# Scratch values kept in PSUM and block pairs mirrored in the head loop of a two-block transformer kernel

## The chip, the cores and the metric

One NeuronCore of a Trainium2 chip runs the kernel. The metric is the device time of one execution in microseconds (us). The engines are TensorE (PE), VectorE (DVE), ScalarE (ACT), GpSimd (POOL) and SyncE (SP), which issues the transfers; SBUF and PSUM are the memories on the chip.

## The reference

256 tokens pass through two transformer blocks of width 1024. The change lies in the second one, in the part that computes, for 16 attention heads of 64 and for 8 recurrent heads of 128:

```python
q = rope(heads(q), pos); k = rope(heads(k), pos)          # t1*cos - t2*sin, t2*cos + t1*sin
p = softmax(where(k_pos <= q_pos, q @ k.T * scale, NEG))   # 256 tokens are one block of the attention
y_a = p @ v
...
fg = lb + (1 - lb) * sigmoid(f);  kh = 1 - fg
b = cumsum(log(fg))                                        # the recurrence in closed form
decay = where(causal, exp(b[t] - b[s]), 0)
a = einsum('td,sd,tsd->ts', silu(q) * dk ** -0.5, kh, decay)
o = a @ i
```

## The kernel before

**The head loop.** The part is a loop of four rounds (`heads2`). A round does four attention heads (two pairs, `j` = 0 to 3) and two recurrent heads (`h` = 0 and 1). Its weights come as 8 chunks of 1 MB, and each chunk gives two output tiles of 128 columns, 16 tiles (`proj(0)` to `proj(15)`), each of 24 matmuls: the weights and the input are split in a high and a low part, ScalarE makes the high part of a chunk in two halves (`ahead2`, L1130), VectorE the low part of the half that is made first (`low_v`, L415) and GpSimd that of the other one (`low_g`, L415).

**The recurrent heads.** The decays between tokens are factored over seven levels, m = 64, 32, ..., 1: within a pair of blocks of m tokens, a key decays to the middle and a query from it. For each level `x` (0 to 6 for head 0, 7 to 13 for head 1) GpSimd writes the differences to the middle (`dl`), ScalarE takes their exponential (`decay`, into `el`, L1429, two buffers), and VectorE multiplies keys (L2027, `kl`) and queries (L2029, `ql`) with it (`level`). TensorE turns them into scores: `hgrn_scores(h, 0)` the diagonal and levels 0 and 1, `(h, 1)` levels 2 to 5, `(h, 2)` level 6 and the product of the two 128-token halves (`cross_level`). A level's scores are block diagonal, and `kl` has zeros for all tokens that are no keys of the level. Every level takes two matmuls, one for each half of the tokens, each with 128 columns of weights and 64 of queries (L930). VectorE puts the scores into the matrix `amat` with predicated copies (`gather0`, `gather1`, `gather2`), and `hgrn_values` multiplies it with the values `iN`.

**The attention heads.** ScalarE copies the tiles of q and k out of PSUM, TensorE multiplies them with a permutation (`rotate`, L894), VectorE applies the sines (`rope_sin`, L2074) and the cosines (`rope_cos`, L2078 and L2079). Then for each head: `scores2` (PE, L903 and L904), `maxima2` (DVE), `exps2` (ACT, L1443 and L1444), `normalise2` (DVE, L2091 to L2093), `turn2` (PE transposes the probabilities, L911), `turned2` (ACT), `values2` (PE).

**What sets the order.** The program of each engine is written out by hand, and an engine does its instructions in that order. Semaphores tie the engines together. `level_ready` counts levels from DVE to PE, `decay_ready` exponentials from ACT to DVE; `turn2(j)` waits for `probs_ready`, and `hgrn_scores(h, 1)` waits until the four levels of its group are done. On TensorE a round stands as: tiles 0 to 5, scores (0, 0), tile 6, rotate q, tile 7, scores (0, 1), rotate k, tile 8, scores (0, 2), tile 9, scores2(0), hgrn_values(0), tile 10, turn2(0), scores2(1), scores (1, 0), tile 11, values2(0), turn2(1), scores2(2), tile 12, scores (1, 1), values2(1), turn2(2), scores2(3), tile 13, scores (1, 2), values2(2), turn2(3), tile 14, hgrn_values(1), values2(3), tile 15.

Of the kernel before, what the change touches and what calls it, by code (L numbers as in the profile page):

```python
# [11 lines left out]
F32 = mybir.dt.float32  # L12
# [6 lines left out]
P = 128  # L19
D = 1024  # L20
KB = D // P
SEQ = 256
# [73 lines left out]
VALUE_BANKS = (6, 2)  # L96
# [68 lines left out]
BODY[('tensor', 'heads2')] = {'roped': 2, 'bank_read7': 4, 'khs_ready': 2, 'level_ready': 16, 'bank_read2': 3, 'bank_read3': 4, 'bank_read4': 4, 'probs_ready': 4, 'bank_read5': 4, 'bank_read6': 1}  # L165
# [3 lines left out]
BODY[('scalar', 'heads2')] = {'bank_full7': 4, 'diff_ready': 14, 'level_ready': 16, 'bank_full4': 4, 'max_ready': 8, 'bank_full3': 4, 'bank_full5': 4, 'bank_full8': 4}  # L169
BODY[('vector', 'heads1')] = {'bank_full4': 4, 'dve_step': 79, 'bank_read4': 4, 'bank_full6': 4, 'conv_ready': 2}  # L170
BODY[('vector', 'up1')] = {'tap0': 8, 'dve_step': 8, 'gate_act': 4}
BODY[('vector', 'heads2')] = {'tanh_ready': 4, 'decay_ready': 16, 'bank_full2': 2, 'dve_step': 22, 'bank_full7': 4, 'bank_read7': 4, 'bank_full3': 4, 'bank_read3': 4, 'bank_full4': 4, 'bank_read4': 4}
# [51 lines left out]
def blocks_kernel(nc, a):  # L224
    ctx = ExitStack()
    with ctx:
# [68 lines left out]
        ones, ident = col("ones", 0, P), col("ident", 0, P)  # L295

# [29 lines left out]
        kh = carve(gluf, 0, HEADS, SEQ)  # L326
        attf = branch[:, :, :].rearrange("p a b -> p (a b)")[:, 2 * KB * TQ:3 * KB * TQ]
# [6 lines left out]
        rope_t = carve(work, 1024, 2, SEQ)  # L334
# [7 lines left out]
        kl = carve(resf, 0, len(LEVELS), SEQ)  # L342
# [3 lines left out]
        el = carve(sqf, 512, 2, SEQ)  # L346
# [39 lines left out]
        meta_shift, meta_exp, meta_probs, meta_T, meta_done = (sem(n) for n in ("meta_shift", "meta_exp", "meta_probs", "meta_T", "meta_done"))  # L386
        att_gated, meta_cleared = sem("att_gated"), sem("meta_cleared")
# [7 lines left out]
        hgrn_ready, tanh_ready, roped = sem("hgrn_ready"), sem("tanh_ready"), sem("roped")  # L395
# [71 lines left out]
        def _(pe):  # L467
# [421 lines left out]
            def rotate(i, src, t):  # L889

                hold(pe, bank_read[2], n.before(bank_read[2]))
                for b in range(2):
                    pe.wait_ge(tile_read[b], STREAM.before("heads2", i, t + b) + 1)
                pe.matmul(ps[:, 2, :], col("rotate", 0, P), src[:, :, :].rearrange("p a b -> p (a b)"),  # L894
                          start=True, stop=True).then_inc(bank_full[2], 1)
# [32 lines left out]
            def level(h, l, bank, at):  # L928
                for blk in range(2):
                    mm = pe.matmul(ps[:, bank, at + HD * blk:at + HD * blk + HD], kl[:, l, blk * P:blk * P + P],  # L930
                                   ql[:, l, blk * HD:blk * HD + HD], start=True, stop=True)
                return mm

            def hgrn_scores(h, g):
# [9 lines left out]
                elif g == 1:  # L944
                    hold(pe, bank_read[3], n.before(bank_read[3]))
# [19 lines left out]
            for b in (2, 3):  # L965
                hold(pe, tile_read[b], STREAM.before("branch_a", 0, b))
            with pe.Fori(0, 4) as i:
# [8 lines left out]
                for t in range(6):  # L976
                    proj(t)
                hgrn_scores(0, 0)
# [35 lines left out]
            for b in VALUE_BANKS:  # L1014
                hold(pe, bank_read[b], n.now(bank_read[b]))
# [80 lines left out]
        def _(sc):  # L1096
# [1454 lines left out]
```

## Time and profile before

| | |
|---|---|
| median of 3 runs | 1180.97 us (1180.48 to 1182.16) |
| the profiled execution | 1181.03 us, its span 1179.4 us |
| granted clock of TensorE, mean | 0.988 |
| busy: PE, DVE, ACT, POOL | 1134.6 us (96%), 720.4 (61%), 600.3 (51%), 651.6 (55%) |
| the chain that ended last | PE 75%, DVE 10%, issue 7%, POOL 5%, ACT 3% |

The span is that of the profiled execution; its own time is the span and 1.6 us around it. Times in the rows are counted from the start of the span. A group of instructions stands with its line, its engine and its operation, out<-in by the names of the memory regions: `work` holds q, k and the probabilities, `res` holds `kl`, `sq` holds `ql`, `dl` and `el`, `glu` the keys `kh`, `act` the matrix `amat`, `ps` is PSUM. An fp32 matmul stands as two records, so that x16 for L930 are eight matmuls; the split products of L570 are one record each.

### The profile page before, as it was taken

What the parts mean: (1) busy time and instruction counts of PE and PEld (TensorE: products, weight loads), DVE (VectorE), ACT (ScalarE), POOL (GpSimd) and SP (SyncE); (2) the same over time, 40 slices, a digit from 0 to 9 for tenths busy, and PEclk for the clock granted to TensorE, in tenths of its full rate; (3) what the DMA queues carried; (4) which work ended last, traced back from release to release, by engine and by line L of the source; (5) the groups of instructions that cost most, each with busy time, mean ns of one, the idle gap of its engine ahead of it and who ended that gap; (6) DMA issues with size and microseconds to landing.
All of it is one profiled execution on the core that took longest, in us unless ns stands there. A gap on an engine that the chain in (4) does not pass through costs nothing.

```text
span 1179.4 us, 24897 instructions
## 1 busy us (share of the span) xinstructions
PE 1134.6 (96%) x8962; PEld 1092.2 (93%) x8962; DVE 720.4 (61%) x1364; ACT 600.3 (51%) x1112; POOL 651.6 (55%) x453
## 2 busy tenths in 40 slices
PE   6999999999889999999899999999999999999997
PEld 6999999998779999999899989898989989999996
DVE  5675766789647777426775757666666546444322
ACT  5654444455256666437545455554635455444332
POOL 5666767660255666544753637364475437656642
PEclk9999999999989999999999999999999999999998
DMA  8444443441344555543432423333445425555541
GB/s 325 144 154 141 171 141 143 143 152 69 142 179 144 178 178 178 199 159 108 178 143 109 142 107 115 134 129 122 160 161 179 143 103 184 181 181 202 185 143 36
DMA packets 26209, 179.43 MB, mean 152 GB/s; under 512 B 2848, under 2 KB 4128, under 8 KB 4768
## 3 DMA queue, kind: packets, MB, share of 16 engines
q1 hardware_dynamic: 25856, 178.28, 42.1%
q8 instruction: 43, 0.70, 0.2%
q10 hardware_dynamic: 288, 0.27, 0.1%
q14 instruction: 22, 0.18, 0.0%
HBM read 177.49 MB, written 1.05 MB: 151 GB/s over the span
## 4 chain that ended last, share of the span: by engine, by line
PE 75%; DVE 10%; issue 7%; POOL 5%; ACT 3%; DVEq 0%; DMA 0%; POOLq 0%; ACTq 0%
PE ps L570 50%; PE ps L852 10%; POOL parts L415 3%; PE ps L930 2%; PE ps L636 1%; DVE ps L2186 1%; DVE act L1824 1%; PE ps L485 1%; ACT parts L1130 1%; DVE branch L1965 1%; PE ps L923 1%; POOL sq L2316 1%; PE ps L610 1%; POOL res L2411 1%; DVE work L1731 1%
## 5 line engine op out<-in xcount | busy, mean ns | idle before, releaser
L415 POOL TENSOR_TENSOR parts<-ring,parts 128x1024 fp32r<-128x1024 f32 x208 | 513.8, 2481 | 468.7 <-ACT parts L1130 465.8
L570 PE MATMUL ps<-x_high,parts 128*128 128x256 f32 (+2 forms) x3088 | 418.0, 284 | 4.3 <-POOL parts L415 2.2
L570 PEld LDWEIGHTS ps<-x_high,parts 128*128 128x128 f32 x3088 | 387.5, 189 | 15.5 <-issue 7.1
L1130 ACT ACTIVATE parts<-ring 128x1024 fp32r<-128x1024 f32 x324 | 323.9, 1049 | 138.3 <-PE ps L852 69.3
L415 DVE TENSOR_TENSOR parts<-ring,parts 128x1024 fp32r<-128x1024 f32 x116 | 152.6, 1315 | 127.3 <-ACT parts L1130 127.3
L570 PE MATMUL ps<-x_low,parts 128*128 128x256 f32 (+2 forms) x1520 | 214.5, 284 | 0.0
L570 PEld LDWEIGHTS ps<-x_low,parts 128*128 128x128 f32 x1520 | 196.3, 189 | 0.0
L1751 DVE SCALAR_TENSOR_TENSOR ps<-glu,table_sb,ps 128x256 f32<-128x256 f32 x232 | 93.3, 481 | 0.6 <-DVE ps L1751 0.3
L852 PE MATMUL ps<-act_high,parts 128*128 128x256 f32 x704 | 87.8, 279 | 0.0
L852 PEld LDWEIGHTS ps<-act_high,parts 128*128 128x128 f32 x704 | 85.1, 188 | 0.0
L570 PE MATMUL ps<-parts,x_high 128*128 128x256 f32 x448 | 62.3, 285 | 0.9 <-DVE work L2099 0.9
L570 PEld LDWEIGHTS ps<-parts,x_high 128*128 128x128 f32 x448 | 56.4, 188 | 3.0 <-issue 3.0
L1109 ACT ACTIVATE work<-ps 128x256 f32<-128x256 f32 (+2 forms) x52 | 20.0, 386 | 74.9 <-PE ps L570 71.9
L852 PE MATMUL ps<-act_low,parts 128*128 128x256 f32 x352 | 46.5, 282 | 0.0
L852 PEld LDWEIGHTS ps<-act_low,parts 128*128 128x128 f32 x352 | 43.8, 189 | 0.0
L1100 ACT ACTIVATE work<-work 128x256 f32<-128x256 f32 x44 | 18.3, 418 | 49.0 <-DVE work L2276 33.0
L1100 ACT ACTIVATE work<-ps,table_sb 128x256 f32<-128x256 f32 x44 | 24.5, 559 | 33.3 <-PE ps L570 29.6
L1965 DVE TENSOR_TENSOR branch<-work 128x256 f32 (+1 forms) x22 | 34.4, 1563 | 3.8 <-DVE work L1960 2.3
L2434 POOL TENSOR_TENSOR sq<-conv 128x128 f32 x56 | 25.6, 457 | 19.6 <-ACT sq L1429 16.0
L1100 ACT ACTIVATE sq<-res 128x256 f32<-128x256 f32 (+2 forms) x48 | 18.2, 412 | 34.9 <-DVE res L1874 27.6
L485 PE MATMUL ps<-conv,ring 128*128 128x258 f32 x128 | 30.4, 399 | 3.5 <-DVE x_high L1837 3.5
L2027 DVE TENSOR_TENSOR res<-glu,sq 128x128 f32<-128x128 f32 x56 | 31.4, 560 | 3.8 <-ACT sq L1429 2.6
(333 smaller groups left out, 1602.2 us busy)
## 6 DMA issues: line engine op xcount, KB each, us to landing
ring<-weights SPq DMA_DIRECT2D x166, 1024.0 KB, 4.8
res<-h_in SPq DMA_DIRECT2D x4, 272.0 KB, 3.6
act<-mem SPq DMA_DIRECT2D x1, 1024.0 KB, 14.6
out<-xT SPq DMA_DIRECT2D x4, 256.0 KB, 2.4
table_sb<-table SPq DMA_DIRECT2D x1, 969.5 KB, 8.9
table_sb<-table ACTq DMA_DIRECT2D x1, 132.5 KB, 3.5
work<-positions ACTq DMA_DIRECT2D x1, 128.0 KB, 5.5
```

The costliest lines, as they stand in the source:

```text
L415: eng.tensor_tensor(parts[:, LOW - HIGH + p, cols], ring[:, slot, cols], parts[:, p, cols].bitcast(F32), ALU.subtract)\
L485: mm = pe.matmul(ps[:, b, 0:width], ring[:, slot, k * CW + e * P:k * CW + e * P + P], moving(k), start=k == 0, stop=k == KB - 1)
L570: mm = pe.matmul(out, left(k), right(k), start=step_ == 0 and k == 0, stop=step_ == 2 and k == KB - 1)
L852: mm = pe.matmul(ps[:, DOWN_BANK + t // 2, t % 2 * SEQ:(t % 2 + 1) * SEQ], w[:, kk * D + t * P:kk * D + t * P + P], x[:, kb + kk, 0:SEQ], ...
L930: mm = pe.matmul(ps[:, bank, at + HD * blk:at + HD * blk + HD], kl[:, l, blk * P:blk * P + P], ql[:, l, blk * HD:blk * HD + HD], start=Tru ...
L1100: ins = sc.activation(out, src, fn, **kw)
L1109: sc.activation(out, src, fn, scale=scale).then_inc(tile_read[b], 1)
L1130: sc.activation(parts[:, p, cols], ring[:, slot, cols], ACT.Copy).then_inc(split_high, 1)
L1751: ve.scalar_tensor_tensor(acc, u, w, acc, ALU.mult, ALU.add).then_inc(dve_step, 1)
L1965: ve.tensor_tensor(branch[:, j + (e - 2), 0:SEQ], silu_g[:, 2 * (g % 2) + e - 2, :], acc, ALU.mult)\
L2027: ve.tensor_tensor(halves(kl[:, l, :], m)[:, :, 0, :], halves(kh[:, i * 2 + h, :], m)[:, :, 0, :], e[:, :, 0, :], ALU.mult)
L2434: gp.tensor_tensor(d[:, :, 0, :], middle, b[:, :, 0, :], ALU.subtract)
```

## The change

- **Mirrored levels.** The second 128 tokens of the keys are written in reversed order, so that the keys of both halves of a level fill one block of 128 tokens without zeros. A level takes one matmul with 128 columns of queries. VectorE writes the keys in two instructions of 64 elements (L2050 and L2051 of the changed kernel) and the queries in one of 128 (L2052).
- So that values stand in the same order, TensorE multiplies the second half of `iN` with a reversed identity (`mirror_values`, after tile 4), and ScalarE copies it back. ScalarE makes `kh_s` in four instructions of 128 elements instead of two of 256.
- **PSUM.** The exponentials of the decays go to PSUM bank 2, which is one buffer (`el` was two): an exponential waits until the level before it is done. The rotated halves are multiplied with the sines in PSUM (bank 6), all of the rope in one piece (`rope`). The exponentials of the attention heads stay in PSUM bank 4.
- **Order.** On TensorE tile 9 stands ahead of scores (0, 2), and tile 10 ahead of `hgrn_values(0)`. On VectorE `rope(q_r)` and `gather0` stand ahead of level 5, `low_v` of chunk 6 between `maxima2(0)` and `normalise2`, level 13 and `cross_level` ahead of `normalise2` of head 2, `gather1` ahead of that of head 3, and `cumulate` at the end.
- GpSimd's clearing of `kl` before the loop falls away. VectorE makes the mirrored masks and the two identities once, between two low parts of the phase `down1`, with 15 small instructions.

```diff
-VALUE_BANKS = (6, 2)
+VALUE_BANKS = (6, 6)
+DECAY_BANK, TURN_BANK = 2, 6
...
+            def mirror_values(i):
+
+                b = STREAM.bank("heads2", 3)
+                hold(pe, bank_read[TURN_BANK], n.before(bank_read[TURN_BANK]))
+                pe.wait_ge(tile_read[b], STREAM.before("heads2", i, 3) + 1)
+                pe.matmul(ps[:, TURN_BANK, 0:CW], both_diagonals[:, P:2 * P], iN[:, 1, :], start=True, stop=True)\
+                  .then_inc(values_mirrored, 1)
...
             def level(h, l, bank, at):
-                for blk in range(2):
-                    mm = pe.matmul(ps[:, bank, at + HD * blk:at + HD * blk + HD], kl[:, l, blk * P:blk * P + P],
-                                   ql[:, l, blk * HD:blk * HD + HD], start=True, stop=True)
-                return mm
+                return pe.matmul(ps[:, bank, at:at + P], kl[:, l, :], ql[:, l, :], start=True, stop=True)
...
-                for t in range(6):
+                for t in range(5):
                     proj(t)
+                mirror_values(i)
+                proj(5)
                 hgrn_scores(0, 0)
...
                 proj(8)
+                proj(9)
                 hgrn_scores(0, 2)
-                proj(9)
                 scores2(0)
+                proj(10)
                 hgrn_values(0)
-                proj(10)
                 turn2(0)
...
                 sc.wait_ge(diff_ready, n.next(diff_ready))
-                reuse(x)
-                sc.activation(el[:, x % 2, :], dl[:, x % 2, :], ACT.Exp).then_inc(decay_ready, 1)
+                reuse(0)
+                sc.activation(ps[:, DECAY_BANK, 0:SEQ], dl[:, x % 2, :], ACT.Exp).then_inc(decay_ready, 1)
...
-                e = halves(el[:, x % 2, :], m)
-                ve.tensor_tensor(halves(kl[:, l, :], m)[:, :, 0, :], halves(kh[:, i * 2 + h, :], m)[:, :, 0, :],
-                                 e[:, :, 0, :], ALU.mult)
+                e, keys = halves(ps[:, DECAY_BANK, 0:SEQ], m), halves(kh[:, i * 2 + h, :], m)
+                b = P // (2 * m)
+                ve.tensor_tensor(halves(kl[:, l, :], m)[:, :, 0, :], keys[:, 0:b, 0, :], e[:, 0:b, 0, :], ALU.mult)
+                ve.tensor_tensor(halves(kl[:, l, :], m)[:, ::-1, 1, ::-1], keys[:, b:, 0, :], e[:, b:, 0, :], ALU.mult)
...
-            def rope_sin(bank):
-                ve.wait_ge(bank_full[bank], n.next(bank_full[bank]))
-                ve.tensor_tensor(rope_t, ps[:, bank, :].rearrange("p (a t) -> p a t", t=SEQ), wide(sin), ALU.mult)\
-                  .then_inc(bank_read[bank], 1)
-
-            def rope_cos(x):
-                step(ve.tensor_tensor(x, x, wide(cos), ALU.mult))
-                ve.tensor_tensor(x, x, rope_t, ALU.add).then_inc(roped, 1)
+            def rope(x):
+                z = ps[:, TURN_BANK, :].rearrange("p (a t) -> p a t", t=SEQ)
+                ve.tensor_tensor(x, x, wide(cos), ALU.mult)
+                step(ve.tensor_tensor(z, z, wide(sin), ALU.mult))
+                ve.tensor_tensor(x, x, z, ALU.add).then_inc(bank_read[TURN_BANK], 1)
...
                 low_v("heads2", i, 4)
                 level(i, 0, 4)
-                rope_sin(2)
+                ve.wait_ge(rotated, n.next(rotated))
+                rope(q_r)
+                gather0()
                 level(i, 0, 5)
-                gather0()
-                rope_cos(q_r)
+                ve.wait_ge(rotated, n.next(rotated))
+                rope(k_r)
                 level(i, 0, 6)
                 cross_level(i, 0)
                 low_v("heads2", i, 5)
+                level(i, 1, 7)
                 gather1()
-                rope_sin(2)
-                rope_cos(k_r)
-                gather2()
-                level(i, 1, 7)
                 level(i, 1, 8)
-                if scan:
-                    ve.wait_ge(log_ready, 2)
-                    cumulate(i + 1)
+                gather2()
                 maxima2(0)
-                normalise2()
                 low_v("heads2", i, 6)
+                normalise2()
                 maxima2(1)
```

The first place is VectorE between the fourth and the fifth level of head 0. Before, the row of the sines (L2074) is followed by level 5 (L2027 and L2029), the diagonal and the first two predicated copies, and then the cosines:

```order
L2074 TENSOR_TENSOR work<-ps,work 128x512 [waits bank_full2]
L2025 REGISTER_ALU
L2027 TENSOR_TENSOR res<-glu,sq 128x64x2 [waits decay_ready]
L2029 TENSOR_TENSOR sq<-work,sq 128x128
L221 REGISTER_ALU
L2050 REGISTER_ALU [waits bank_full3]
L2051 TENSOR_TENSOR act<-ps,table_sb 128x256 [waits bank_full7]
L1639 ISA
L2043 COPY_PREDICATED act<-table_sb,ps 128x2x64 [waits dve_step]
L2046 REGISTER_ALU
L2043 COPY_PREDICATED act<-table_sb,ps 128x4x32 [waits dve_step]
L2078 TENSOR_TENSOR work<-work 128x512 [waits bank_read7]
```
In the changed kernel the whole rope of q (L2096 to L2098) and `gather0` (L2074 and L2066) come first:

```order
L2096 TENSOR_TENSOR work<-work 128x512 [waits rotated]
L2097 TENSOR_TENSOR ps<-ps,work 128x512
L1649 ISA
L2098 TENSOR_TENSOR work<-work,ps 128x512 [waits dve_step]
L222 REGISTER_ALU
L2073 REGISTER_ALU [waits bank_full3]
L2074 TENSOR_TENSOR act<-ps,glu 128x256 [waits bank_full7]
L1649 REGISTER_ALU
L2066 COPY_PREDICATED act<-table_sb,ps 128x2x64 [waits dve_step]
L2069 REGISTER_ALU
L2066 COPY_PREDICATED act<-table_sb,ps 128x4x32 [waits dve_step]
L2047 REGISTER_ALU [waits bank_read7]
```
The last row opens level 5, whose three products (L2050 to L2052) follow it; they have moved behind two more products of 512 elements, one of 256 and two predicated copies.

The second place is VectorE at the first attention head. Before, the maxima (L2084 to L2087) are followed by the probabilities (L2091 to L2093) and those by the low part of chunk 6 (L415):

```order
L2082 REGISTER_ALU
L2084 TENSOR_TENSOR ps<-ps,table_sb 128x2x128 [waits bank_full4]
L1639 REGISTER_ALU
L2086 TENSOR_REDUCE small<-ps 128x1 [waits dve_step]
L2087 TENSOR_REDUCE small<-ps 128x1
L2090 REGISTER_ALU
L2091 RECIPROCAL small<-small 128x2 [waits bank_read4]
L1639 REGISTER_ALU
L2092 TENSOR_SCALAR work<-work,small 128x128 [waits dve_step]
L2093 TENSOR_SCALAR work<-work,small 128x256
L414 ISA
L415 TENSOR_TENSOR parts<-ring,parts 128x1024 [waits split_high]
```
In the changed kernel the low part (L417) stands between them:

```order
L2101 REGISTER_ALU
L2103 TENSOR_TENSOR ps<-ps,table_sb 128x2x128 [waits bank_full4]
L1649 REGISTER_ALU
L2105 TENSOR_REDUCE small<-ps 128x1 [waits dve_step]
L2106 TENSOR_REDUCE small<-ps 128x1
L416 ISA
L417 TENSOR_TENSOR parts<-ring,parts 128x1024 [waits split_high]
L2109 REGISTER_ALU
L2110 RECIPROCAL small<-small 128x2 [waits bank_read4]
L1649 REGISTER_ALU
L2111 TENSOR_SCALAR work<-ps,small 128x128 [waits dve_step]
L2112 TENSOR_SCALAR work<-ps,small 128x256
```
The row that waits for `split_high`, the high part of chunk 6, has moved ahead of the rows that `turn2(0)` waits for.

## Rows read from the trace of the kernel before

**Rows 1.** Busy time by stretch (us): one round of the head loop.

```profile
649.40:714.80 65.40, 65.40 (x511) 60.61 (x510) 43.43 (x99) 34.99 (x77) 32.91 (x37) 1.00 0.36 128
```

**Rows 2.** The chain that ended last, head loop: start us, us, engine, line, records.

```profile
635.94 20.10 PE ps L570 x168
656.04 0.44 PE ps L940 x4
...
663.90 1.73 PE ps L930 x16
...
673.74 0.63 PE ps L960 x2
...
701.30 20.10 PE ps L570 x168
```

**Rows 3.** Timeline of TensorE, one round: start us, us, engine, line, operation.

```profile
660.05 1.02 PE L894 MATMUL ps<-work,table_sb 128*128 128x512 f32 x2
...
663.74 1.89 PE L930 MATMUL ps<-sq,res 128*128 128x64 f32 x16
...
672.82 0.48 PE L903 MATMUL ps<-work 64*128 64x128 f32 x2
...
677.28 0.49 PE L911 MATMUL ps<-table_sb,work 128*128 128x128 f32 x3
...
690.62 0.55 PE L911 MATMUL ps<-table_sb,work 128*128 128x128 f32 x3
...
696.46 0.55 PE L911 MATMUL ps<-table_sb,work 128*128 128x128 f32 x3
```

**Rows 4.** Timeline of VectorE, same round.

```profile
661.11 0.69 DVE L2074 TENSOR_TENSOR work<-ps,work 128x512 f32<-128x512 f32 x1 [1.72 <-PE ps L894]
...
662.46 0.41 DVE L2051 TENSOR_TENSOR act<-ps,table_sb 128x256 f32<-128x256 f32 x1
...
663.82 0.69 DVE L2078 TENSOR_TENSOR work<-work 128x512 f32<-128x512 f32 x1
664.54 0.78 DVE L2079 TENSOR_TENSOR work<-work 128x512 f32<-128x512 f32 x1
665.24 0.28 DVE L2027 TENSOR_TENSOR res<-glu,sq 128x128 f32<-128x128 f32 x1
665.45 0.28 DVE L2029 TENSOR_TENSOR sq<-work,sq 128x128 f32<-128x128 f32 x1
...
673.97 0.41 DVE L2084 TENSOR_TENSOR ps<-ps,table_sb 128x256 f32<-128x256 f32 x1
...
676.01 0.17 DVE L2091 RECIPROCAL small<-small 128x2 f32<-128x2 f32 x1 [0.98 <-ACT work L1444]
...
676.41 0.35 DVE L2093 TENSOR_SCALAR work<-work,small 128x256 f32<-128x256 f32 x1
676.96 1.23 DVE L415 TENSOR_TENSOR parts<-ring,parts 128x1024 fp32r<-128x1024 f32 x1 [0.20 <-ACT parts L1130]
...
696.04 1.77 DVE L2043 COPY_PREDICATED act<-table_sb,ps 128x128 f32<-128x128 int32 x4
```

**Rows 5.** Timeline of ScalarE, same round.

```profile
660.53 0.41 ACT L1429 ACTIVATE sq<-sq 128x256 f32<-128x256 f32 x1
...
675.07 0.37 ACT L1443 ACTIVATE work<-ps,small 128x128 f32<-128x128 f32 x1 [1.75 <-DVE small L2087]
...
675.87 2.00 ACT L1130 ACTIVATE parts<-ring 128x1024 fp32r<-128x1024 f32 x2
```

**Rows 6.** Timeline of all engines, same round: GpSimd beside VectorE.

```profile
652.75 2.49 POOL L415 TENSOR_TENSOR parts<-ring,parts 128x1024 fp32r<-128x1024 f32 x1 [1.50 <-ACT parts L1130]
...
653.63 1.76 DVE L2027 TENSOR_TENSOR res<-glu,sq 128x128 f32<-128x128 f32 x1 [0.64 <-ACT sq L1429]
...
659.61 2.38 POOL L415 TENSOR_TENSOR parts<-ring,parts 128x1024 fp32r<-128x1024 f32 x1
```

**Rows 7.** Timeline of VectorE in the phase down1.

```profile
489.14 1.23 DVE L415 TENSOR_TENSOR parts<-ring,parts 128x1024 fp32r<-128x1024 f32 x1 [4.45 <-ACT parts L1130]
```

More of the change, by code:

```diff
@@ L889, in rotate @@
             def rotate(i, src, t):
[L891 removed]
+                hold(pe, bank_read[TURN_BANK], n.before(bank_read[TURN_BANK]))
                 for b in range(2):
                     pe.wait_ge(tile_read[b], STREAM.before("heads2", i, t + b) + 1)
[L894 to L895 removed]
+                pe.matmul(ps[:, TURN_BANK, :], col("rotate", 0, P), src[:, :, :].rearrange("p a b -> p (a b)"),
+                          start=True, stop=True).then_inc(rotated, 1)
+            def mirror_values(i):
+                b = STREAM.bank("heads2", 3)
+                hold(pe, bank_read[TURN_BANK], n.before(bank_read[TURN_BANK]))
+                pe.wait_ge(tile_read[b], STREAM.before("heads2", i, 3) + 1)
+                pe.matmul(ps[:, TURN_BANK, 0:CW], both_diagonals[:, P:2 * P], iN[:, 1, :], start=True, stop=True)\
+                  .then_inc(values_mirrored, 1)
             def scores2(j):
@@ L900, in scores2 @@
                 if j == 0:
-                    pe.wait_ge(roped, n.next(roped, 2))
+                    hold(pe, bank_read[TURN_BANK], n.now(bank_read[TURN_BANK]))
                 hold(pe, bank_read[4], n.before(bank_read[4]))
@@ L1013, in _ @@
             last_products = split_late("branch_a", ya_high, ya_low, SEQ, None, 2)
-            for b in VALUE_BANKS:
-                hold(pe, bank_read[b], n.now(bank_read[b]))
+            hold(pe, bank_read[VALUE_BANKS[1]], n.now(bank_read[VALUE_BANKS[1]]))
             last_products()
@@ L1507, in _ @@
                 copy2(9, vA[:, 1, :])
+                decay(8)
                 exps2(0)
@@ L2134, in heads2 @@
                 low_v("heads2", i, 5)
+                level(i, 1, 7)
                 gather1()
-                rope_sin(2)
-                rope_cos(k_r)
+                level(i, 1, 8)
                 gather2()
-                level(i, 1, 7)
-                level(i, 1, 8)
+                maxima2(0)
+                low_v("heads2", i, 6)
+                normalise2()
+                maxima2(1)
+                gather0()
+                normalise2()
+                for x in range(9, 13):
+                    level(i, 1, x)
+                maxima2(2)
+                level(i, 1, 13)
+                cross_level(i, 1)
+                normalise2()
+                low_values(i, 0)
+                low_v("heads2", i, 7)
+                maxima2(3)
+                gather1()
+                normalise2()
+                gather2()
                 if scan:
@@ L2143, in heads2 @@
                     cumulate(i + 1)
-                maxima2(0)
-                normalise2()
-                low_v("heads2", i, 6)
-                maxima2(1)
-                normalise2()
-                gather0()
-                for x in range(9, 13):
-                    level(i, 1, x)
-                maxima2(2)
-                normalise2()
-                level(i, 1, 13)
-                cross_level(i, 1)
-                low_values(i, 0)
-                low_v("heads2", i, 7)
-                maxima2(3)
-                normalise2()
-                gather1()
-                gather2()
                 low_v("heads2", i, 8)
```

57 lines of the change are left out of this document (33 added, 24 removed).

## The prediction

> **What bounds the kernel now.** I first read the busy time by stretch. One round of the head loop shows TensorE busy for 65.40 of 65.40 us at a granted clock of 1.00, VectorE for 43.43, ScalarE for 34.99 and GpSimd for 32.91 [rows 1]. Then the chain that ended last: it stays on TensorE through the loop, and the same piece stands at 635.94 and at 701.30, so a round is 65.36 us [rows 2]. All that VectorE, ScalarE and GpSimd do is covered, and a change pays only through TensorE's own work. The question is then how far ahead of TensorE the others are, which only the timelines tell. VectorE is busy without a gap from 661.11, when the rotated q has come, to the end of the maxima of head 0 at 675.03, just before ScalarE takes them up at 675.07; head 0's probabilities are done at 676.41 + 0.35 = 676.76, and TensorE uses them at 677.28 [rows 3 to 5]. That is 0.5 us of slack in a round of 65.
>
> **What TensorE saves.** Group (h, 1) is eight matmuls of 64 columns in 1.73 us, 0.216 each; a matmul of 128 columns costs the same, two of them in 0.44 us [rows 2]. So the weights set the price, and one matmul for two saves 0.21 us per level. 14 levels save 2.94 us a round. `mirror_values` adds a matmul of 256 columns. The product of that width stands in a piece of 0.63 us that holds its start [rows 2]; the bounds are 0.43 (half of the 512 columns that L894 takes in 0.86) and 0.63, and I take 0.5. Net: 2.4 us a round saved, 9.8 us over four rounds, if TensorE still never waits. It reads `iN` one whole tile (20.10 us for seven, 2.87 [rows 2]) after tile 3, which ScalarE copies at once, so that this matmul itself waits for nothing.
>
> **Where it will wait.** I lay the new program over the round of the rows, with the durations of its rows, and keep their clock.
>
> Early levels. The single buffer turns a level into a round trip: exponential 0.41 [rows 5], products 0.56 (0.14 + 0.14 + 0.28; two products of 128 start 0.21 apart [rows 4], so that one of 64 takes 0.14), and two hand-overs of 0.03: about 1.04 us. Levels 0 to 4 have the gaps for it, level 4 being done near 659.8, and group (0, 0) has over 3 us of slack.
>
> Level 5. TensorE now arrives at group (0, 1) at 663.8, as before at 663.74 [rows 3] (0.5 added, 0.4 saved). The rotated q reaches VectorE near 661.2. Then come the cosines, the sines and the sum (0.61 to 0.72 each, 2.0 together, from L2074, L2078 and L2079), `gather0` (from 662.46 to 663.82, 1.36) and level 5 (0.55): done 3.9 us after 661.2, at 665.1, if nothing is in its way. That alone is a wait of 1.3 us.
>
> But the cosines are a product of two SBUF operands. Such a product, started at 653.63 while GpSimd was in its low part of 652.75 to 655.24, took 1.76 us instead of 0.28, till just behind its end [rows 6]. L2074, which has one operand in PSUM, took its normal 0.69 in the middle of the low part of 659.61 to 661.99 [rows 4, 6]. The new level products are of that free kind, the cosines are not. GpSimd's low part of chunk 4 waits behind a difference that waits for the exponential of level 4, and comes at about 660.1 to 662.5. The cosines end at 662.5 + 0.5, the sum and `gather0` at 665.7, level 5 at 666.3. TensorE waits 2.4 us (bounds 1.2 and 2.6). Behind that wait stands `rotate` of k, for which VectorE waits in turn.
>
> Head 0. `rotate` ends by 668.3. GpSimd's next low part, behind the difference that needs level 5's successor, starts near 667.6, so the cosines of k are held until 670.1 too. Rope ends at 672.0; level 6 and `cross_level` (1.0) are just ahead of TensorE, which comes to (0, 2) at 673.8. Then `low_v` 1.15, level 7 0.55, `gather1` 1.8 (four copies in 1.77 [rows 4]), level 8 0.55, `gather2` 0.7: VectorE begins `maxima2(0)` at 677.75 and ends at 678.85. The scores have been there since 675.1. From the end of the maxima the old trace took 0.98 us to the probabilities' first row (676.01) and 0.75 more to their end. Now the low part of chunk 6 is between, and it waits for the high part, which ScalarE makes only behind those exponentials: from 675.03 (end of the maxima) to 676.96 (start of L415) are 1.93 us [rows 4, 5], L415 costs 1.15, `normalise2` 0.75: 3.8 us. Probabilities at 682.7. TensorE is at `turn2(0)` at 678.75 and waits 3.9 us. The bound from below: were VectorE free when the scores come, as it was, the path is 1.1 + 3.8 = 4.9 us against the 3.6 that TensorE has to do between (677.28 less 672.82 + 0.85 [rows 3]), so that 1.4 us stay in any case.
>
> Second half, counted from `turn2(0)` as T. Head 1 is in time: probabilities at T + 4.6, wanted at T + 5.9. Levels 9 to 12 at one per 1.04 us end at T + 8.3, which is when the scores of head 2 are just there (T + 7.2); `maxima2(2)` follows to 9.4, exponentials 10.35, and then level 13 and `cross_level`, which ScalarE can feed only now, stand ahead of `normalise2`: T + 12.5, wanted at T + 11.9 (before 690.62 less 677.28, 13.3 [rows 3], now 1.3 to 1.4 less for six saved matmuls of 0.21). Wait 0.6, bounds 0 and 1.0. For head 3 the low part of chunk 7 (VectorE free at T + 14.1, held by GpSimd's to 15.6, done 16.7), the maxima to 17.7, `gather1` 1.85 behind them instead of the 0.95 of the exponentials, and `normalise2`: T + 20.3. TensorE is there at T + 18.1 (696.46 less 677.28 [rows 3], 19.2, less seven times 0.21 and a little, plus the 0.6). Wait 2.2, bounds 0.8 (the low part not held) and 2.5.
>
> Sum: waits 2.4 + 3.9 + 0.6 + 2.2 = 9.1 us a round, less 2.4 saved, 6.7 more; four rounds 26.8. Against the profiled execution's own 1181.03 us, which is the median of the runs within 0.1, that is 1207.8.
>
> Edits at nothing: the exponentials and probabilities in PSUM are as long as before (L2074 with PSUM and L2078 without both take 0.69 us for 512 elements [rows 4]). The 15 instructions in `down1`, at 0.2 to 0.3 us like other short rows, are some 4 us in a stage where VectorE waits 4.45 us between two low parts [rows 7]; without that cover they would cost up to 4 us once. Four ScalarE copies for two add 0.4 us at a place where `decay(2)` has room. The clearing of `kl` was before the loop and beside TensorE's products.
>
> One rule of the Trainium skill speaks against the change. "VectorE: DVE Perf Modes", its section on the TRN2 errata, gives an instruction from PSUM a fixed 120 cycles and one from SBUF 58. By it an estimate is 0.065 us more for each product that now reads PSUM, twelve of which stand between the rope of q and `maxima2(0)`: 0.8 us a round more, 1211. The rows of equal length above say otherwise, and I go by them.
>
> **The rivals.** *The ports don't matter (15%).* If GpSimd's low parts fall elsewhere, the cosines are free. Then level 5 is done at 665.1, a wait of 1.2; VectorE ends `maxima2(0)` at about 675.9, which makes 2.2 at `turn2(0)`; 0.6 and 0.8 behind: 4.8 less 2.4, 2.4 a round, 1191. For it: a shift of 1 us decides each of the three. Against it: each of the low parts hangs on what VectorE and ScalarE did just before.
>
> *Both near their lower bounds (7%).* 1.2 and 1.4 and nothing behind are 2.6 against 2.4: no change, 1181 to 1183.
>
> *Faster (11%).* VectorE is fast enough after all. The point that decides is level 5 by 663.8 and probabilities within 3.6 us of the scores. It takes products of 64 elements and ropes in PSUM that are much shorter than their relatives in the rows, 3.9 us falling to 2.6. Nothing in the rows speaks for it, but it would give all that TensorE saves: 1171.
>
> *Worse (7%).* The waits push ScalarE's high parts too, which I have behind TensorE's needs by a microsecond or two only at chunk 0 of the next round: another 1 to 3 us a round, 1212 to 1220.
>
> **How the numbers follow.** My forecast, 1195 to 1212, has 60%; its likeliest is 1208. The waits' bounds alone would give from 1.2 + 1.4 to 2.6 + 4.2 + 1.0 + 2.5 = 10.3 less 2.4, 1182 to 1213. The range that leaves out less than 2 in 10 is 1184 to 1214: it takes in the second case and leaves the faster one, most of the unchanged one and half of the worse one. A measurement of this kernel tells about 0.2%, 2.4 us, from no change. Slower by more than that: 60 + 15 + 7 and nothing of the rest, 0.82; within it 0.07; faster 0.11.
>
> **What would show it.** In the changed kernel L939 stands as 112 matmul records of 128 columns, a group of four in about 0.88 us. Rows in which TensorE is idle until VectorE: at group (0, 1) on the products of level 5, and at the transposes of the probabilities on L2112, in every round, the latter the longest. L2096 should have members well over 0.69 us, L2050 to L2052 none over 0.3. A round is 72 us instead of 65.4. I am wrong if TensorE is gapless in the loop, or if the idle time lies at the start of tiles, on weights' parts.

## The result, and the profile after

The changed kernel takes 1219.18 us (median of 4 runs, 1216.15 to 1221.96) against 1181.07 (1180.48 to 1182.16): ratio 1.0314, 95% interval 1.0287 to 1.0341. It is slower by 38 us; 27 were forecast. Its profiled execution took 1216.15 us (span 1214.5, mean granted clock 0.973).

Busy time by stretch, one round of the changed kernel (as [rows 1]: PE, PEld, DVE, ACT, POOL, granted clock, share of the DMA engines, GB/s):

```profile
674.73:749.63 74.90, 67.93 (x482) 61.84 (x483) 42.61 (x112) 35.54 (x82) 30.27 (x36) 0.93 0.32 113
```

A round takes 74.90 us against 65.40 [rows 1]. VectorE is busy no longer than before (42.61 against 43.43); TensorE is idle for 6.97 us, and its clock is 0.93 instead of 1.00. The waits of TensorE from 560 to 880 us, in all, times, longest:

```profile
PE ps L921 <- DVE work L2112: 17.4, 8, 2.7
PE ps L939 <- DVE sq L2052: 9.0, 4, 2.3
```

L939 waits for the products of level 5, L921 (the transposes of the probabilities of heads 0 and 3) for L2112, the end of `normalise2`. These are three of the four places that were forecast; at `turn2(2)` TensorE does not wait here. The timeline of TensorE, around the three waits of the round:

```profile
674.73 1.23 PE L939 MATMUL ps<-sq,res 128*128 128x128 f32 x8 [2.27 <-DVE sq L2052]
675.76 1.92 PE L896 MATMUL ps<-work,table_sb 128*128 128x512 f32 x2
676.69 2.63 PE L572 MATMUL ps<-parts,x_high 128*128 128x256 f32 x8
...
688.65 0.38 PE L970 MATMUL ps<-act,work 128*128 128x128 f32 x2
691.69 0.55 PE L921 MATMUL ps<-table_sb,work 128*128 128x128 f32 x3 [2.66 <-DVE work L2112]
...
705.36 0.55 PE L921 MATMUL ps<-table_sb,work 128*128 128x128 f32 x3
...
713.06 0.79 PE L921 MATMUL ps<-table_sb,work 128*128 128x128 f32 x3 [2.04 <-DVE work L2112]
713.50 2.06 PE L572 MATMUL ps<-x_high,parts 128*128 128x256 f32 x8
```

The durations behind the waits have grown. Eight products of L572 take 2.63 us behind the first wait; the same group takes 1.50 us where the clock is full (674.02 in a fence of experiment 5). Busy time by stretch shows why, in its third last column (the first two rows belong to the round before):

```profile
616.00:620.00 4.00, 2.88 (x11) 2.07 (x12) 1.75 (x7) 0.93 (x3) 2.41 (x1) 0.71 0.22 35
620.00:624.00 4.00, 4.00 (x21) 4.00 (x21) 2.64 (x11) 1.19 (x5) 0.81 (x2) 0.50 0.57 229
...
676.00:680.00 4.00, 4.00 (x18) 2.97 (x18) 2.29 (x2) 0.00 (x0) 3.25 (x4) 0.61 0.00 0
680.00:684.00 4.00, 4.00 (x36) 4.00 (x35) 3.82 (x13) 0.69 (x2) 1.09 (x2) 1.00 0.00 0
...
692.00:696.00 4.00, 4.00 (x20) 3.30 (x18) 1.51 (x5) 1.68 (x6) 1.09 (x2) 0.59 0.47 131
...
712.00:716.00 4.00, 2.94 (x15) 2.94 (x16) 3.42 (x11) 2.04 (x3) 0.00 (x0) 0.65 0.50 209
```

Behind each of the three waits TensorE is busy again at a granted clock of 0.50, its lower level of 1.2 GHz, for about 3.4 us in this round, and then returns to 2.4 GHz: 1.7 us of work are lost each time. Behind two waits of the other rounds (2.59 us, ending at 617.12, and 2.32, ending at 839.19) it is nearly 7 us, with 3.4 lost. In the kernel before, the loop has 1.00 throughout, in this round [rows 1] and in the other three: it had no waits.

VectorE and GpSimd around the first two waits:

```profile
669.66 1.77 DVE L2096 TENSOR_TENSOR work<-work 128x512 f32<-128x512 f32 x1 [1.45 <-PE ps L896]
...
674.40 0.28 DVE L2052 TENSOR_TENSOR sq<-work,ps 128x128 f32<-128x128 f32 x1
677.71 2.08 DVE L2096 TENSOR_TENSOR work<-work 128x512 f32<-128x512 f32 x1 [3.04 <-PE ps L896]
...
687.21 0.41 DVE L2106 TENSOR_REDUCE small<-ps 128x1 f32<-128x256 f32 x1
689.55 1.23 DVE L417 TENSOR_TENSOR parts<-ring,parts 128x1024 fp32r<-128x1024 f32 x1 [1.93 <-ACT parts L1137]
...
691.15 0.48 DVE L2112 TENSOR_SCALAR work<-ps,small 128x256 f32<-128x256 f32 x1
```
```profile
668.52 2.37 POOL L417 TENSOR_TENSOR parts<-ring,parts 128x1024 fp32r<-128x1024 f32 x1
...
676.89 2.37 POOL L417 TENSOR_TENSOR parts<-ring,parts 128x1024 fp32r<-128x1024 f32 x1
```

Both cosines (L2096) end just behind a low part of GpSimd, at 671.4 and 679.8. Those of q do so in every round. Those of k take 1.58, 2.08 and 2.27 us in the three rounds in which the clock falls behind the first wait, and 0.73 in the last round, in which it doesn't (the wait of 2.18 us that ends at 824.19). In `normalise2` the low part of chunk 6 waits 1.93 us for ScalarE's high part, exactly as long as was read from before. By form, from 600 to 880 us, cosines, queries' products and the larger product of the normalisation (busy, mean ns, idle before):

```profile
L2096 DVE TENSOR_TENSOR work<-work 128x512 f32<-128x512 f32 x7 | 12.0, 1712 | 15.9 <-PE ps L896 15.9
...
L2052 DVE TENSOR_TENSOR sq<-work,ps 128x128 f32<-128x128 f32 x51 | 14.3, 281 | 0.0
...
L2112 DVE TENSOR_SCALAR work<-ps,small 128x256 f32<-128x256 f32 x16 | 7.6, 476 | 0.0
```

### The profile page after: what moved, and what is told of

It is laid out like the page before. It is cut to its first block, busy times and chain, and to the rows that moved or that the text cites. A ratio compares the mean times of both kernels' runs of the same rounds, so it can differ in the third digit from the quotient of the medians.

```text
span 1214.5 us, 24795 instructions
## 1 busy us (share of the span) xinstructions
PE 1141.6 (94%) x8858; PEld 1095.2 (90%) x8858; DVE 720.6 (59%) x1435; ACT 602.1 (50%) x1124; POOL 639.0 (53%) x452
## 4 chain that ended last, share of the span: by engine, by line
PE 64%; DVE 16%; issue 10%; POOL 5%; ACT 4%; DVEq 1%; DMA 0%; POOLq 0%; ACTq 0%; SPq 0%
PE ps L572 43%; PE ps L854 10%; POOL parts L417 3%; ACT parts L1137 2%; PE ps L638 1%; DVE act L2066 1%; DVE parts L417 1%; DVE ps L2205 1%; DVE act L1834 1%; PE ps L487 1%; PE ps L939 1%; DVE branch L1975 1%; PE ps L896 1%; POOL sq L2335 1%; PE ps L612 1%
## 5 line engine op out<-in xcount | busy, mean ns | idle before, releaser
L417 POOL TENSOR_TENSOR parts<-ring,parts 128x1024 fp32r<-128x1024 f32 x208 | 510.7, 2465 | 468.7 <-ACT parts L1137 465.8
L572 PE MATMUL ps<-x_high,parts 128*128 128x256 f32 (+2 forms) x3088 | 424.5, 287 | 2.8 <-POOL parts L417 2.7
L572 PEld LDWEIGHTS ps<-x_high,parts 128*128 128x128 f32 x3088 | 393.3, 191 | 15.3 <-issue 8.4
L417 DVE TENSOR_TENSOR parts<-ring,parts 128x1024 fp32r<-128x1024 f32 x116 | 155.4, 1340 | 144.5 <-ACT parts L1137 144.5
L572 PE MATMUL ps<-x_low,parts 128*128 128x256 f32 (+2 forms) x1520 | 217.3, 286 | 0.0
L572 PEld LDWEIGHTS ps<-x_low,parts 128*128 128x128 f32 x1520 | 199.4, 192 | 0.0
L572 PE MATMUL ps<-parts,x_high 128*128 128x256 f32 x448 | 64.3, 293 | 3.2 <-DVE work L2118 3.2
L572 PEld LDWEIGHTS ps<-parts,x_high 128*128 128x128 f32 x448 | 58.3, 195 | 7.0 <-issue 6.9
L1436 ACT ACTIVATE ps<-sq 128x256 f32<-128x256 f32 x56 | 21.6, 386 | 46.7 <-DVE res L2058 23.7
```

The source lines that it names most:

```text
L417: eng.tensor_tensor(parts[:, LOW - HIGH + p, cols], ring[:, slot, cols], parts[:, p, cols].bitcast(F32), ALU.subtract)\
L572: mm = pe.matmul(out, left(k), right(k), start=step_ == 0 and k == 0, stop=step_ == 2 and k == KB - 1)
L1436: sc.activation(ps[:, DECAY_BANK, 0:SEQ], dl[:, x % 2, :], ACT.Exp).then_inc(decay_ready, 1)
```

## The experiments

Ratios are to runs of the kernel before on the same chip.

### What a wait costs

**1. The waits filled.** Throwaway matmuls of ones and an identity, 9 ahead of the wait at scores (0, 1), 14 and 8 at `turn2(0)` and `turn2(3)`:

```diff
+                for _ in range({0: 14, 3: 8}.get(j, 0)):
+                    pe.matmul(ps[:, 5, 0:P], ones, ident, start=True, stop=True)
                 pe.wait_ge(probs_ready, n.next(probs_ready))
```

> The changed kernel, with throwaway matmuls (ones times identity, 0.21 us each) that TensorE does in the places where it waits: 9 ahead of the wait of group (0, 1), 14 ahead of turn2(0), 8 ahead of turn2(3), in every round. They write to a bank that the next real matmuls overwrite. Theory 1 (the miss of the forecast is the granted clock, which falls behind each wait and makes about 3.4 us of work twice as long): with the waits filled the clock stays at 1.00 in the loop, a round is 72 to 72.5 us, and the kernel takes 1206 to 1211 us although it does more work. Theory 2 (the waits themselves are longer than I reckoned and the clock is only a by-product): the time stays at 1216 to 1222 or grows by what the extra matmuls cost.

Measured: 1203.72 us (1200.84 to 1206.15), 1.0189 (1.0163 to 1.0214). The loop's clock is 1.00 and a round 70.89 us (level group at 671.62 and 742.51):

```profile
671.62 1.16 PE L941 MATMUL ps<-sq,res 128*128 128x128 f32 x8 [0.28 <-DVE sq L2056]
699.85 0.52 PE L923 MATMUL ps<-table_sb,work 128*128 128x128 f32 x3 [0.46 <-DVE work L2116]
742.51 1.16 PE L941 MATMUL ps<-sq,res 128*128 128x128 f32 x8 [0.28 <-DVE sq L2056]
```

More work for TensorE makes the kernel 15.5 us faster. Two things in the trace refine this. The cosines of k (L2100 here) are free: they start just ahead of GpSimd's low part, and GpSimd is the one that takes longer. And 14 matmuls at `turn2(0)` are more than fit: the probabilities are done at 686.14 + 0.48 = 686.62, and the transposes start at 687.26.

```profile
673.68 0.69 DVE L2100 TENSOR_TENSOR work<-work 128x512 f32<-128x512 f32 x1 [2.11 <-PE ps L896]
...
686.14 0.48 DVE L2116 TENSOR_SCALAR work<-ps,small 128x256 f32<-128x256 f32 x1
```
```profile
673.78 2.86 POOL L417 TENSOR_TENSOR parts<-ring,parts 128x1024 fp32r<-128x1024 f32 x1
```
```profile
687.26 0.49 PE L923 MATMUL ps<-table_sb,work 128*128 128x128 f32 x3
```

In the change the transposes start 0.06 us behind the probabilities (691.63 and 691.69). So about 0.6 us of each filled round is the fillers' own (an estimate from these rows): at full clock a round would take some 70.3 us. Of the 38 us the lowered clock, with the hold of k's cosines that comes with it, is then 15.5 us as measured and some 18 without the fillers' excess. The other 20 are what the waits cost less what TensorE saves.

**2. One of the three filled** (14 matmuls, at `turn2(0)` alone).

> The changed kernel with throwaway matmuls at one of its three waits only: 14 of them ahead of the wait for the first probabilities, none at scores (0, 1) or at the probabilities of head 3. The waits themselves (2.3 and 2.0 us of TensorE) stay at the other two places. The run with one low part moved has just these two waits and a granted clock of 1.00 behind both. Theory A (the clock falls behind two of the waits only because of the third between them): the loop shows a clock of 1.00 and a round of about 70.9 us, 1202 to 1206 us, no slower than with all three filled. Theory B (each wait of 2 us or more brings its own stretch of half clock, and the other run escaped by something else in its order): the stretches behind the two waits stay, 1.7 us each, and the time is 1210 to 1218 us.

Measured: 1215.48 us (1212.45 to 1215.73), 1.0274 (1.0252 to 1.0295): theory B's time. But the clock doesn't fall behind every wait:

```profile
600.00:604.00 4.00, 1.73 (x14) 1.53 (x14) 3.29 (x9) 2.44 (x4) 0.00 (x0) 1.00 0.70 254
604.00:608.00 4.00, 4.00 (x30) 3.52 (x30) 2.12 (x5) 0.68 (x3) 3.49 (x5) 1.00 0.02 8
640.00:644.00 4.00, 4.00 (x24) 4.00 (x22) 2.73 (x6) 2.38 (x3) 1.16 (x1) 0.57 0.07 27
676.00:680.00 4.00, 3.76 (x17) 2.95 (x18) 1.36 (x2) 1.12 (x4) 3.05 (x5) 0.70 0.16 66
```

A wait of 2.27 us that ends at 603.79 leaves the clock at 1.00, one of 2.04 ending at 639.70 lowers it, and the next of 2.27, ending at 676.24, lowers it too. Over the loop three of the four waits at scores (0, 1) leave it alone, and all four at `turn2(3)` lower it. The run prices one fall: the round with one (603.79 to 676.24) takes 72.45 us, the round with two (676.24 to 750.24) 74.00, and the filled one 70.89: 1.55 us each, a little less than the 1.7 us of lost work, since later waits shrink.

**3. The late low part in the kernel before**, alone:

```diff
                 maxima2(0)
-                normalise2()
                 low_v("heads2", i, 6)
+                normalise2()
```

> The kernel before with one edit: the low part of chunk 6 stands between maxima2(0) and normalise2(0). By the rows of before the probabilities then come 2.1 us later (678.85) and TensorE waits 1.6 us in each round. Theory 1 (each wait also costs clock, 1.7 us): 1.6 + 1.7 = 3.3 us a round, 1194 us, and a granted clock under 0.99 in the loop. Theory 2 (a wait costs only itself): 1187.5 us. If the slack is taken up elsewhere: 1181.

Measured: 1206.43 us (1205.19 to 1211.14), 1.0221 (1.0192 to 1.0251). One moved line costs 25.4 us, and 13 were expected. VectorE, then GpSimd, then TensorE:

```profile
685.55 1.23 DVE L415 TENSOR_TENSOR parts<-ring,parts 128x1024 fp32r<-128x1024 f32 x1 [1.93 <-ACT parts L1130]
...
686.89 2.17 DVE L2092 TENSOR_SCALAR work<-work,small 128x128 f32<-128x128 f32 x1
```
```profile
686.54 2.43 POOL L415 TENSOR_TENSOR parts<-ring,parts 128x1024 fp32r<-128x1024 f32 x1 [6.04 <-ACT parts L1130]
```
```profile
689.38 0.90 PE L911 MATMUL ps<-table_sb,work 128*128 128x128 f32 x3 [3.34 <-DVE work L2093]
```

Both terms were larger than expected. L2092, with one input and one output in SBUF, is held until GpSimd's low part ends (2.17 us, a mean of 0.29 before), so that the wait is 3.34 us and not 1.6. Behind it the clock is 0.59 and 0.56 for two stretches of 4 us (688 to 696), which loses about 3 us of work and not 1.7.

**4. The same with 15 throwaway matmuls** at `turn2(0)`.

> The kernel before with the low part of chunk 6 ahead of normalise2(0), as in e5_before_low6 (1206.4 us, one wait of 3.34 us a round, granted clock 0.95), plus 15 throwaway matmuls (3.2 us) that TensorE does in place of that wait. If the wait costs itself and the clock behind it the rest: clock 1.00, a round 65.4 + 3.5 = 68.9 us, 1195 us. If the clock is no part of the price: 1206 us.

Measured: 1196.08 us (1195.15 to 1198.76), 1.0115 (1.0093 to 1.0138), the loop's clock 1.00. A round takes 68.99 us against 71.79 in experiment 3. The medians are 10.4 us apart; this run was on another chip, where the kernel before takes 1182.54 us, so that 13.5 of the 25.4 us are left and the clock is 10 to 12.

### Which piece of the order

**5. Low part of chunk 6 back** behind `normalise2` of head 0, in the changed kernel, alone.

> The changed kernel with the low part of chunk 6 put back behind the normalisation of head 0, nothing else. Theory: the wait of 2.7 us at the first transposes falls under 1 us, the waits at scores (0, 1) and of head 3 stay: 2 to 4 us a round less, 1203 to 1211 us. Rival (the low part is only exchanged for another delay at head 3 or at tile 12): less than 1 us a round, 1215 us or more.

Measured: 1195.61 us (1194.84 to 1197.84), 1.0121 (1.0105 to 1.0137), 23.6 us off the change. A round is 68.27 us (672.57 to 740.84), 6.6 less. The wait that shrinks, from 2.66 to 0.29 us, is only 2.4 of them; the rest is the clock:

```profile
672.57 1.16 PE L939 MATMUL ps<-sq,res 128*128 128x128 f32 x8 [2.28 <-DVE sq L2052]
...
674.02 1.50 PE L572 MATMUL ps<-parts,x_high 128*128 128x256 f32 x8
675.36 1.11 PE L572 MATMUL ps<-parts,x_low 128*128 128x256 f32 x8
...
685.53 0.55 PE L921 MATMUL ps<-table_sb,work 128*128 128x128 f32 x3 [0.29 <-DVE work L2112]
...
705.78 0.55 PE L921 MATMUL ps<-table_sb,work 128*128 128x128 f32 x3 [2.03 <-DVE work L2112]
```
```profile
672.00:676.00 4.00, 3.43 (x24) 2.96 (x25) 1.85 (x6) 1.45 (x4) 2.71 (x5) 1.00 0.24 100
...
708.00:712.00 4.00, 4.00 (x30) 3.50 (x30) 1.99 (x3) 1.98 (x4) 2.46 (x1) 1.00 0.00 0
```

Two waits stay, as long as before, and now the clock keeps 1.00 behind both, in all four rounds. Why it does here, and not behind waits as long in the change, no run shows.

**6. Level 5 back** ahead of the rope of q, in the changed kernel, alone.

> The changed kernel with level 5 put back ahead of the rope of q, nothing else. Theory (waits add, and each costs its own length and the half clock behind it): the wait of 2.3 us at scores (0, 1) goes with its 1.7 us of clock, the wait at the first transposes stays near 2.7 us: 3 to 4 us a round less, 1203 to 1208 us. Rival (VectorE is the bound of this stretch, so a wait removed early comes back at the transposes): the wait there grows to over 4 us and the time is 1213 us or more.

Measured: 1210.75 us (1207.06 to 1212.26), 1.0236 (1.0218 to 1.0255), between the times of the two theories. The wait at scores (0, 1) is gone, and the one at `turn2(0)` has grown from 2.66 to 4.01, with half clock for nearly 7 us behind it in three of the four rounds. The lateness is VectorE's: a wait that TensorE no longer has early comes back later. And a hold has moved on: with the cosines of k free (0.69 us), the product of `cross_level` took their place beside a low part of GpSimd:

```profile
678.87 2.49 DVE L2058 TENSOR_TENSOR res<-work,res 128x128 f32<-128x128 f32 x1
```

**7. Both.**

> The changed kernel with two pieces of VectorE's order put back: level 5 ahead of the rope of q, and the low part of chunk 6 behind normalise2(0). Theory 1 (the order on VectorE makes the waits): the wait at group (0, 1) is gone, that at turn2(0) falls to 1.4 us or less, those of the second half stay; 1187 us if the clock cost nothing, 1192 to 1200 with it. Theory 2 (the single buffer of the exponentials makes VectorE late, the order matters little): over 1208 us.

Measured: 1195.79 us (1193.15 to 1201.16), 1.0139 (1.0104 to 1.0173), no faster than 5 alone: the wait of 2.28 at scores (0, 1) has become one of 1.93 at `turn2(0)`, with the clock lowered behind it.

**8. GpSimd's low parts of chunks 4 and 5 one difference earlier.**

```diff
-                for x in (0, 1, "low 2", 2, 3, "low 3", 4, 5, 6, "low 4", 7, 8, "low 5", 9, 10, "low 6", 11, 12, 13,
+                for x in (0, 1, "low 2", 2, 3, "low 3", 4, 5, "low 4", 6, 7, "low 5", 8, 9, 10, "low 6", 11, 12, 13,
```

> The changed kernel with GpSimd's low parts of chunks 4 and 5 one difference earlier in its order, so that they lie ahead of the ropes. Theory 1 (a product of two SBUF operands is held until GpSimd's low part ends): L2096 falls from 1.77 and 2.08 us to 0.7 to 1.3, the wait at group (0, 1) from 2.3 to about 1.4, the one at turn2(0) by about 1, the whole to 1208 to 1213 us. Theory 2 (the ports don't matter, L2096 is slow for another reason): L2096 as long as before, 1216 to 1222 us.

Measured: 1210.13 us (1205.96 to 1211.05), 1.0248 (1.023 to 1.0265).

```profile
666.91 0.79 DVE L2096 TENSOR_TENSOR work<-work 128x512 f32<-128x512 f32 x1 [1.45 <-PE ps L896]
...
673.04 0.90 DVE L2096 TENSOR_TENSOR work<-work 128x512 f32<-128x512 f32 x1 [2.11 <-PE ps L896]
```
```profile
673.36 2.86 POOL L417 TENSOR_TENSOR parts<-ring,parts 128x1024 fp32r<-128x1024 f32 x1
```

With GpSimd elsewhere the cosines are free, and the wait at scores (0, 1) falls from 2.27 to 1.29 us: the hold was about 1 us of that wait, and VectorE's order the rest. The wait at `turn2(0)` was expected to shrink by about 1 us and is 3.00: counted from TensorE's coming to scores (0, 1), the probabilities are ready 2.3 us earlier in the round than in the change, but TensorE comes 2.6 us earlier, since it waits less and its clock has not fallen.

**9. The second half's order undone too** (both pieces of 7, `normalise2` of head 2 and `gather1` of head 3 at their old places; the values in PSUM as in the change).

> The changed kernel with five pieces of VectorE's order put back: level 5 first, low part of chunk 6 behind normalise2(0), normalise2 of head 2 ahead of level 13, and normalise2 of head 3 ahead of gather1. The exponentials stay in one PSUM buffer. Theory 1 (order): the wait at turn2(3) falls from 1.64 us to 0.8 or less, that at turn2(0) stays near 1.9 with its clock cost; 1185 to 1191 us. Theory 2 (single buffer): the waits of the second half stay because levels 9 to 12 are late; 1195 us as with two pieces put back.

Measured: 1196.02 us (1191.71 to 1196.63), 1.01 (1.0076 to 1.0124); 1185 to 1191 was expected. The wait at `turn2(3)` is still 1.75 us, about as long as in 7 (1.64): ahead of it the low part of chunk 7 runs 2.53 us (700.69 to 703.2) instead of 1.2, since it starts inside GpSimd's (699.75 to 702.13).

### Where the values lie, and an order that fits

**10 and 11. One order, two places.** An order of my own (on VectorE level 5 ahead of the rope, `low_v` of chunk 5 and `gather1` ahead of the rope of k, `normalise2` right behind the maxima of heads 0 and 2, `low_v` of chunk 7 ahead of the low part of the values, `normalise2` of head 3 ahead of `gather1`). ScalarE's order is part of it. The change had also put the copy of tile 7 and the high part of chunk 3 ahead of the exponentials of level 6 and `cross_level`, and the exponential of level 8 behind the copies of tiles 8 and 9, which the section on the change does not list; here both are undone, and no run tests them alone. The order came first with the exponentials of the decays in two buffers in SBUF:

> Mirrored levels with an order of my own: exponentials in SBUF with two buffers as before the change, level 5 ahead of the rope, low part of chunk 5 and gather1 ahead of the rope of k, normalise2 right behind the maxima of heads 0 and 2, low part of chunk 7 ahead of low_values(0), normalise2 of head 3 ahead of gather1. If mirroring is worth what I reckoned (2.4 us a round) and no wait is left: TensorE gapless, a round of 62.9 to 63.2 us, 1171 to 1173 us. If one wait with its clock cost is left: 1175 to 1185.

Measured: 1194.34 us (1191.51 to 1198.16), 1.0097 (1.0075 to 1.0119). The same with them in PSUM, one buffer:

```diff
-                reuse(x)
-                sc.activation(el[:, x % 2, :], dl[:, x % 2, :], ACT.Exp).then_inc(decay_ready, 1)
+                reuse(0)
+                sc.activation(ps[:, DECAY_BANK, 0:SEQ], dl[:, x % 2, :], ACT.Exp).then_inc(decay_ready, 1)
```

> The same order as in e8_best, but the exponentials in the one PSUM buffer of the changed kernel. If the single buffer costs nothing once the order is right: 1171 to 1173 us as the other. If its round trip of about 1.0 us a level puts levels 6 to 8 and 9 to 12 late: one or two waits of 0.5 to 1.5 us, 1180 to 1195 us.

Measured: 1180.45 us (12 runs, 1174.72 to 1183.09) against 1182.54, 0.9972 (0.9956 to 0.9988). The products of the keys, by form, with SBUF (first fence) and with PSUM:

```profile
L2052 DVE TENSOR_TENSOR res<-glu,sq 128x64 f32<-128x64 f32 x51 | 25.1, 493 | 0.0
L2051 DVE TENSOR_TENSOR res<-glu,sq 128x64 f32<-128x64 f32 x50 | 23.1, 463 | 5.2 <-ACT sq L1437 4.9
```
```profile
L2050 DVE TENSOR_TENSOR res<-glu,ps 128x64 f32<-128x64 f32 x50 | 10.9, 219 | 17.9 <-ACT ps L1436 17.6
L2051 DVE TENSOR_TENSOR res<-glu,ps 128x64 f32<-128x64 f32 x50 | 10.7, 215 | 0.0
```

So it pays to have the exponentials of the decays in PSUM: the products take 463 to 493 ns with both operands in SBUF, 215 to 219 with one in PSUM. The medians are 13.9 us apart, although PSUM has one buffer and SBUF two. Part of that is clock again: with SBUF TensorE waits 2.35 to 2.45 us at scores (0, 2), and behind three of the four waits the clock falls. A round is 66.92 us where it doesn't fall (672.14 to 739.06) and 69.23 where it does, against 64.23 in PSUM.

**12. The order moved once more** (on VectorE level 6 and `cross_level` ahead of `low_v` of chunk 5 and the rope of k, level 8 behind `maxima2(0)`; within the rope the sines ahead of the cosines; on ScalarE the exponential of level 8 at its place of the change).

> The order of the best run, with VectorE's pieces moved once more so that level 6 and the cross level stand ahead of the rope of k, level 8 behind the maxima of head 0. Theory: what is left of TensorE's idle time in that run (0.56 us at scores (0, 2), 0.35 us at tile 10) is VectorE's and ScalarE's order alone; without it a round is 62.9 to 63.3 us and the time 1171 to 1176 us. Rival: a wait of up to 0.6 us stays, or moves to the probabilities of head 0, where GpSimd's low part holds the cosines of k (2.2 us in place of 0.7): 1178 to 1181 us.

Measured: 1174.59 us (6 runs, 1170.42 to 1176.63) against 1181.15, 0.9939 (0.9922 to 0.9955): faster than both kernels. Busy time by stretch, one round:

```profile
664.54:727.24 62.70, 62.70 (x485) 57.82 (x483) 39.46 (x113) 35.58 (x80) 32.54 (x37) 1.00 0.38 134
```

No gap is left, and the round is 65.36 less 62.70 = 2.66 us shorter than before. The sines, which have one operand in PSUM, now run beside GpSimd's low part (0.70 us at 661.91), and the cosines of q behind them take 1.18 us instead of 1.78. Which of the moves closed the last gaps was not tested one by one. Four rounds are 10.6 us, the median 6.6. Most of the rest lies where the loop begins: behind a wait of 3.37 us that ends at 580.14 half clock loses 2.7 us, and from 500 to 580 us this kernel's clock is 0.95 against 0.98. The kernel before had two shorter waits there (2.03 and 0.88), and its clock stayed at 1.00 behind them.

## Why the prediction was wrong

The direction and the places of the waits were right (the smallest, at `turn2(2)`, shows only at full clock), the size was not: 1219.2 lies above 1208 and above the range's 1214. By its steps:

- **"Waits 2.4 + 3.9 + 0.6 + 2.2 = 9.1 us a round."** This is the step that failed: it counts a wait at its own length and leaves TensorE's clock at 1.00 ("with the durations of its rows, and keep their clock"). Filled, the round is 70.89 us (experiment 1), some 0.6 of them the fillers' own; as it stands, 74.90. The difference is the clock and what follows from it, 4.0 to 4.6 us a round, 15.5 us in all as measured and some 18 without the fillers' excess. With this term the forecast would have been 1223 to 1226, above the result: a second, smaller error ran the other way.
- **The waits one by one.** Three were sized well, as experiment 2 shows them: 2.27 at scores (0, 1) (2.4 said), 0.46 at `turn2(2)` (0.6), 2.05 at `turn2(3)` (2.2). The fourth, at `turn2(0)`, was sized too long: at full clock it is about 2.4 us (684.30, the end of the product ahead of the fillers in experiment 1, to 686.7; 2.32 in the last round of the change), and 3.9 were said. The prediction let GpSimd hold the cosines of k too. At full clock they begin 0.1 us ahead of GpSimd's low part and are free (0.69); they are held only where the clock has fallen and `rotate` of k comes late. At full clock a round of some 70.3 us is 4.9 more than before, about 1201 us in all, and the sum said 1208. That the forecast came within 11 us of the result is in part luck: 7 us too much at `turn2(0)` and elsewhere stood against the 18 of the clock.
- **"TensorE saves 2.4 us a round"**: 2.66, shown by the round without gaps (experiment 12).
- **The cosines of q held by GpSimd**: shown. L2096 has a mean of 1712 ns where the row of before has 733 (L2078, by form, the same stretch of the program), 0.7 to 0.9 when GpSimd was moved (8). The first rival, that the ports don't matter, is out.
- **The low part of chunk 6 as the longest wait**: shown. It alone is 23.6 us (5), and put into the kernel before it is 25.4 (3).
- **"Edits at nothing: the exponentials and probabilities in PSUM are as long as before"**: right for products of two operands (0.69 for 512 elements in L2097 and L2098), wrong for the normalisation: L2111 and L2112 take 0.35 and 0.48 us, L2092 and L2093 took 0.29 and 0.35. 0.2 us for each head, ahead of each `turn2`. The Trainium skill has this in "VectorE: DVE Perf Modes", "Mode 2×_2P": an operation with a single SBUF source and an SBUF destination can fetch two elements at once, and a PSUM operand excludes that. The trace agrees (0.06 us more for 128 elements, 0.13 for 256). The errata table of the same page, which the prediction had weighed, is not seen for two operands.
- **The "worse" rival** gave 1212 to 1220 and so named the time, but by ScalarE's high parts, and these brought no wait of TensorE in the loop. The cause was another.

**What stays open** is when the clock falls. Inside the loops it never fell behind a wait of 1.3 us or less. Above that, length does not decide it. Of the waits of about 3 us and more one left the clock at 1.00 (3.00 us in experiment 8, ending at 758.64), where waits of 2.99 and 3.00 in the same run lowered it. In experiment 10 one of 2.45 us lowered it and the next of 2.45 (ending at 681.40) did not. Of waits of 2.0 to 2.3 us, four in the change lowered it and one of 2.18 did not, three of eight in experiment 2 did not, nor did any of the eight in experiment 5. 1.93 us did in experiment 7 and not in 9, 1.75 us in 9 did, and 1.64 us in 7 did not. Ahead of the loop, where the program is the same, a wait of 3.16 to 3.19 us left the clock alone in the change and in experiment 1 and lowered it in experiment 2. Theory A of experiment 2, that a third wait is what brings it down, fell. The runs give the price of a fall and no rule for it, and a profile shows one execution of each kernel.

## What to carry to other kernels

Where TensorE has no gap, a wait is not priced at its length: take 1.6 to 3.4 us more of lost clock as possible for one of 2 to 3 us, and try throwaway matmuls in the gap to see which share is the clock's. A hand-written order has to be laid over the other engines' holds, since a piece moved between a result and its consumer costs its own time, the input it waits for, and whatever GpSimd then holds. Judge placement and order apart: here the placement in PSUM and the mirrored levels gave 0.6% in an order that fits them, and the order that came with them lost nearly 4% against it.

## What the runs showed of the hardware

- An operation of VectorE with a single tensor input is held by GpSimd too where input and output lie in SBUF (the TENSOR_SCALAR of L2092, 2.17 us instead of 0.29). And the hold goes both ways: in experiment 8 the low part of GpSimd that began at 673.36, inside VectorE's cosines, took 2.86 us instead of 2.37. "SBUF — State Buffer" of the Trainium skill, "SBUF: two separate sides", has both: whoever starts first keeps the shared ports for the whole instruction, and the modes with two ports count as well as two SBUF inputs.
- More matmuls made the kernel faster, twice: 15.5 us with 31 a round, some 10 us with 15.
